# A two-layer hybrid decoder step: weight granules multiplied in three fp32r products, or once in float32

## What is computed

```python
for l in range(DEPTH):                                   # DEPTH = 2
    x = layer_norm(DN_ALPHA * x + 0.5 * swiglu(x, ffn1_w_in[l], ffn1_w_out[l]), ln1_g[l], ln1_b[l])
    proj = x @ w_in[l]                                   # 1024 x 2696
    f_r, f_s, f_g = jnp.split(proj, [R_PROJ, R_PROJ + S_PROJ], axis=-1)
    y_r = rwkv7_mixer(f_r, ...); y_s = swa(f_s, ...); y_g = gdn_mixer(f_g, ...)
    mix = jnp.concatenate([y_r, y_s, y_g], axis=-1) @ w_out[l]      # 1024 x 1024
    x = layer_norm(DN_ALPHA * x + mix, ln2_g[l], ln2_b[l])
    x = layer_norm(DN_ALPHA * x + 0.5 * swiglu(x, ffn2_w_in[l], ffn2_w_out[l]), ln3_g[l], ln3_b[l])
# swiglu: gate, up = split(x @ w_in (1024 x 5632)); (silu(gate) * up) @ w_out (2816 x 1024)
```

## Time and profile before

| | |
|---|---|
| median of 3 runs | 3039.74 us (3028.84 to 3040.9) |
| the profiled execution's own time | 3037.87 us |
| its span, first to last instruction | 3036.1 us |
| PE busy | 2744.6 us, 90% |
| DVE busy | 1652.3 us, 54% |
| ACT busy | 941.4 us, 31% |
| mean granted TensorE clock | 0.896 |

### The profile page before, as it was taken

How to read it: one execution, slowest core, us unless ns; L and a number is a source line. 1 busy time by engine, 2 the same in 40 slices (tenths; PEclk the granted TensorE clock), 3 DMA queues, 4 the chain that set the end, 5 groups by cost and what they waited for, 6 DMA issues and landing times.

```text
span 3036.1 us, 59313 instructions
## 1 busy us (share of the span) xinstructions
PE 2744.6 (90%) x23248; PEld 2565.4 (84%) x23248; DVE 1652.3 (54%) x2489; ACT 941.4 (31%) x1679; POOL 179.6 (6%) x186
## 2 busy tenths in 40 slices
PE   8999999978787799999999999998887688999995
PEld 8999998856565699999999999987665567999994
DVE  5666346745555356663366643565555543666533
ACT  4333233322212133332233332343222212433322
POOL 1030110000000020001100001000000002000010
PEclk9999999977676699999999999998686768999997
DMA  4842334200000223232222222421000012223221
GB/s 110 99 90 87 88 114 113 56 8 1 9 9 5 72 77 90 83 90 85 84 79 88 85 86 87 130 91 32 5 9 1 9 38 80 77 83 90 86 85 47
DMA packets 381441, 201.60 MB, mean 66 GB/s; under 512 B 41381, under 2 KB 378789, under 8 KB 380472
## 3 DMA queue, kind: packets, MB, share of 16 engines
q1 hardware_dynamic: 378872, 197.46, 22.6%
q0 software_dynamic: 2400, 1.82, 1.8%
HBM read 188.07 MB, written 13.34 MB: 66 GB/s over the span
## 4 chain that ended last, share of the span: by engine, by line
PE 80%; DVE 10%; issue 5%; ACT 4%; SPq 1%; DMA 0%; DVEq 0%; ACTq 0%; POOLq 0%; POOL 0%
PE ps L656 55%; PE ps L710 22%; DVE ar L1805 3%; DVE ar L1799 2%; ACT ar L1336 2%; SPq L517 1%; PE ps L1059 1%; PE ps L964 1%; ACT wh L1267 1%; DVE wl L1683 1%; DVE x L1713 0%; DVE x L1799 0%; DVE ar L1835 0%; DVE x L1711 0%; DVE xl L1790 0%
## 5 line engine op out<-in xcount | busy, mean ns | idle before, releaser
L1683 DVE TENSOR_TENSOR wl<-raws,wh 128x1024 fp32r<-128x1024 f32 x332 | 406.5, 1225 | 734.5 <-ACT wh L1267 730.5
L656 PE MATMUL ps<-xh,wh 128*128 128x272 f32 x3136 | 662.7, 293 | 43.8 <-DVE xl L1799 18.2
L656 PE MATMUL ps<-xh,wl 128*128 128x272 f32 x3136 | 656.3, 291 | 0.0
L656 PE MATMUL ps<-xl,wh 128*128 128x272 f32 x3136 | 654.8, 290 | 0.0
L710 PE MATMUL ps<-ar 64*64 64x64 f32 (+13 forms) x4984 | 495.3, 294 | 122.8 <-ACT ar L1336 38.2
L710 PEld LDWEIGHTS ps<-ar 64*64 64x64 f32 (+5 forms) x4984 | 370.1, 179 | 223.4 <-issue 64.0
L656 PEld LDWEIGHTS ps<-xh,wh 128*128 128x128 f32 x3136 | 502.1, 192 | 49.7 <-issue 26.5
L656 PEld LDWEIGHTS ps<-xl,wh 128*128 128x128 f32 x3136 | 502.0, 191 | 0.0
L656 PEld LDWEIGHTS ps<-xh,wl 128*128 128x128 f32 x3136 | 501.1, 191 | 0.0
L1267 ACT ACTIVATE wh<-raws 128x1024 fp32r<-128x1024 f32 x332 | 350.6, 1057 | 455.9 <-PE ps L656 430.6
L656 PE MATMUL ps<-hh,wh 128*128 128x272 f32 x1408 | 292.2, 289 | 0.0
(11 more groups left out here) (188 smaller groups left out, 2755.2 us busy)
## 6 DMA issues: line engine op xcount, KB each, us to landing
raws<-in_ffn_w_in SPq DMA_DIRECT2D x176, 512.0 KB, 3.7
raws<-in_ffn_w_out SPq DMA_DIRECT2D x64, 512.0 KB, 4.0
raws<-in_w_in SPq DMA_DIRECT2D x42, 512.0 KB, 3.6
raws<-in_ffn_w_out SPq DMA_DIRECT2D x32, 384.0 KB, 3.4
raws<-in_w_out SPq DMA_DIRECT2D x16, 512.0 KB, 4.1
x_kept<-x SPq DMA_DIRECT2D x2, 2176.0 KB, 10.2
x<-x_kept SPq DMA_DIRECT2D x2, 2176.0 KB, 7.9
ar<-in_consts SPq DMA_DIRECT2D x2, 1337.5 KB, 6.5
```

The costliest lines, as they stand in the source:

```text
L656: ins = pe.matmul(ps[:, bank + h, 0:n1 - h * NH], w[u % 2][:, k, :], a[:, k0 + k, h * NH:n1], start=(first and k == 0 and n == 0), stop=(l ...
L1683: dve.tensor_tensor(wl[u % 2][:, :, :], raw[u % 2][:, :, :], wh[u % 2][:, :, :].bitcast(F32), ALU.subtract).then_inc(sem("wl_done"), 1)
```

## The change

All granules and activations are plain float32. `raws` becomes a ring of four load buffers (`SLOTS`), TensorE reads the weights there and waits for the load itself; `wh`, `wl`, `xl`, `hl` and all code that makes them are gone. SP waits on `mm_done` of the granule that used the slot before. The mixer's input counts two granules that do not exist (`SKIP`), so that each stage begins at slot 0; the first two granules of `w_out` are loaded right after the last of the mixer's input, into slots 0 and 1, since odd head pairs keep rows in slots 2 and 3. `keep_busy` is taken out. DVE writes `hh` and the last step of each head straight into `xh`. FFN loops of SP and TensorE are unrolled to multiples of four granules.

```diff
-        xh = sb("xh", [P, KC, NX], F32R)
-        xl = sb("xl", [P, KC, NX], F32R)
-        raws = sb("raws", [P, 2, 8, P])
+        xh = sb("xh", [P, KC, NX])
+        raws = sb("raws", [P, SLOTS, 8, P])
...
             def load(lay, g, u, src):
-                sp.wait_ge(sem("wl_done"), at(lay, "wl_done", g + u - 1))
-                sp.dma_start(raw[u % 2][:, 0:src.shape[1], 0:src.shape[2]], src).then_inc(raw_in[u % 2], 16)
+                slot = u % SLOTS
+                sp.wait_ge(sem("mm_done"), at(lay, "mm_done", g + u - SLOTS + 1))
+                sp.dma_start(raw[slot][:, 0:src.shape[1], 0:src.shape[2]], src).then_inc(raw_in[slot], 16)
...
-            def granule(lay, g, u, nblocks, hi, lo, k0, bank, first, last, split_from=None):
-                pe.wait_ge(sem("wl_done"), at(lay, "wl_done", g + u + 1))
+            def granule(lay, base, n, u, nblocks, a, k0, bank, first, last, split_from=None):
+                slot = u % SLOTS
+                pe.wait_ge(raw_in[slot], (lay * slot_uses(NG, slot) + slot_uses(base, slot) + n + u // SLOTS + 1) * 16)
                 for k in range(nblocks):
                     if split_from is not None:
-                        pe.wait_ge(sem("xl_done"), at(lay, "xl_done", split_from + k + 1))
-                    for n, (w, a) in enumerate(((wh, hi), (wh, lo), (wl, hi))):
-                        for h in range(2):
-                            n1 = a.shape[2] if h else NH
-                            ins = pe.matmul(ps[:, bank + h, 0:n1 - h * NH], w[u % 2][:, k, :], a[:, k0 + k, h * NH:n1],
-                                            start=(first and k == 0 and n == 0), stop=(last and k == nblocks - 1 and n == 2))
+                        pe.wait_ge(sem("xh_done"), at(lay, "xh_done", split_from + k + 1))
+                    for h in range(2):
+                        n1 = a.shape[2] if h else NH
+                        ins = pe.matmul(ps[:, bank + h, 0:n1 - h * NH], raw[slot][:, k, :], a[:, k0 + k, h * NH:n1],
+                                        start=(first and k == 0), stop=(last and k == nblocks - 1))
...
-                def keep_busy(p, n):
-                    if p.q == 3:
-                        for _ in range(n):
-                            pe.matmul(ps[:, 3, 0:NH], xh[:, 2, 0:P], xh[:, 3, 0:NH], start=True, stop=True)
...
-            def split(lay, g, u):
-                n = g + u
-                act.wait_ge(raw_in[u % 2], lay * (NG // 2 * 16) + g * 8 + (u // 2) * 16 + 16)
-                act.wait_ge(sem("mm_done"), at(lay, "mm_done", n - 1))
-                act.activation(wh[u % 2][:, :, :], raw[u % 2][:, :, :], ACT.Copy).then_inc(sem("wh_done"), 1)
...
-            def split(lay, g, u):
-                dve.wait_ge(sem("wh_done"), at(lay, "wh_done", g + u + 1))
-                dve.wait_ge(sem("mm_done"), at(lay, "mm_done", g + u - 1))
-                dve.tensor_tensor(wl[u % 2][:, :, :], raw[u % 2][:, :, :], wh[u % 2][:, :, :].bitcast(F32),
-                                  ALU.subtract).then_inc(sem("wl_done"), 1)
...
-                tt(xl[:, 2:6, 0:SEQ], y_attn[:, :, 0:SEQ], xh[:, 2:6, 0:SEQ].bitcast(F32), ALU.subtract).then_inc(*tick("attn_l"))
...
-                        stt(y, y, 0.5, U[:, ZG, :], ALU.mult, ALU.mult).then_inc(*tick("y_final"))
+                        if q == 3:
+                            dve.wait_ge(sem("x_back"), at(lay, "x_back", 16))
+                        stt(final, y, 0.5, U[:, ZG, :], ALU.mult, ALU.mult).then_inc(*tick("head_l"))
...
-                    if q == 3:
-                        split(lay, BASE_WO, 0)
-                    dve.wait_ge(sem("head_h"), at(lay, "head_h", q + 1))
-                    ch = q if q < 2 else 4 + q
-                    tt(xl[:, ch, 0:NT], y, xh[:, ch, 0:NT].bitcast(F32), ALU.subtract).then_inc(*tick("head_l"))
```

More of the change, by code:

```diff
@@ L46 @@
 N_FFN_IN, N_FFN_OUT = 2 * FC, 3 * KC
+SLOTS = 4
+SKIP = -PC % SLOTS
 BASE_F1I = 0
@@ L49 @@
 BASE_PJ = BASE_F1O + N_FFN_OUT
-BASE_WO = BASE_PJ + PC
+BASE_WO = BASE_PJ + PC + SKIP
 BASE_F2I = BASE_WO + KC
@@ L53, with slot_uses @@
 NG = BASE_F2O + N_FFN_OUT
+assert all(b % SLOTS == 0 for b in (BASE_F1O, BASE_PJ, BASE_WO, BASE_F2I, BASE_F2O, NG))
+def slot_uses(base, slot):
+    return base // SLOTS - (base >= BASE_WO and slot >= SLOTS - SKIP)
 LAST_ROW = P - 1
@@ L265, in trunk @@
         x = sb("x", [P, KC, NT])
-        xh = sb("xh", [P, KC, NX], F32R)
-        xl = sb("xl", [P, KC, NX], F32R)
-        raws = sb("raws", [P, 2, 8, P])
[L269 to L273, removed]
+        xh = sb("xh", [P, KC, NX])
+        raws = sb("raws", [P, SLOTS, 8, P])
+        raw = [raws[:, s] for s in range(SLOTS)]
         gram_odd = sb("gram_odd", [P, GRAM_W])
@@ L334, in trunk @@
         passed = sem("passed")
-        raw_in = [sem("raw_in0"), sem("raw_in1")]
+        raw_in = [sem(f"raw_in{k}") for k in range(SLOTS)]
         for name in START:
@@ L556, in one_layer @@
                     load_proj(g)
+                for u in range(2):
+                    load(lay, BASE_WO, u, columns(w_mix, lay, (0, KC), u * P))
                 def put(dst, src, name="states_out"):
@@ L611, in one_layer @@
                         put(out("p_" + name, lay)[:, 0, 2 * c + hp, :, :].rearrange("a m n -> (a m) n"), src, "state_out")
-                with sp.Fori(1, KC // 2) as c:
-                    for u in range(2):
-                        load(lay, BASE_WO + c * 2, u, columns(w_mix, lay, (0, KC), c * (2 * P) + u * P))
+                for u in range(4, KC):
+                    load(lay, BASE_WO, u, columns(w_mix, lay, (0, KC), u * P))
+                    sp.sem_inc(passed, 1)
                 ffn_weights(lay, 1, BASE_F2I)
@@ L717, in proj_part @@
                         pe.sem_inc(passed, 1)
-                        pe.wait_ge(sem("wl_done"), at(lay, "wl_done", BASE_PJ + g + 1))
+                        pe.wait_ge(raw_in[g % SLOTS], (lay * slot_uses(NG, g % SLOTS) + slot_uses(BASE_PJ, g % SLOTS) + g // SLOTS + 1) * 16)
                     for k in range(k0, k1):
[L720 to L724, removed]
+                        for h in range(2):
+                            n1 = NX if h else NH
+                            ins = mm(ps[:, 2 * u + h, 0:n1 - h * NH], raw[g % SLOTS][:, k, :], xh[:, k, h * NH:n1],
+                                     start=(k == 0), stop=(k == KC - 1))
                     if k1 == KC:
-                        ins.then_inc(sem("mm_done"), 1)
+                        ins.then_inc(sem("mm_done"), 1 + SKIP if g == PC - 1 else 1)
                 def turn_caches():
@@ L1303, in ffn @@
                 g_cols(lay, 2 * ph, lay + (LN_SLOT[1] if ph == 0 else 1))
[L1305 to L1314 removed]
+                with act.Fori(0, KC // 2) as d:
+                    for u in range(2):
+                        squares(lay, 2 * ph, d * 2, u)
+                        z_high(lay, 2 * ph, lay + (LN_SLOT[1] if ph == 0 else 1), d * 2 + u)
             def g_cols(lay, n, slot):
                 act.wait_ge(sem("lnp_in"), 16 * LN_DMAS)
[L1319 removed]
+                act.activation(xh[:, :, NT:NX], affine_cols(slot), ACT.Copy)
             def squares(lay, n, c, u):
```

198 lines of the change are left out of this document (58 added, 140 removed).

## The result

| | before | changed |
|---|---|---|
| median | 3036.35 us (4 runs, 3028.84 to 3040.9) | 3380.16 us (4 runs, 3368.36 to 3384.87) |
| ratio, 95% interval | | 1.1129 (1.1091 to 1.1168) |
| the profiled execution, its span | 3037.87 us, 3036.1 us | 3380.69 us, 3378.8 us |

A forecast was written before the change was run, and what follows sets the result against it. The prediction took TensorE, 90% busy and without gaps in the FFN stages, as the bound. Its terms, +417 - 23 - 27 - 20 = +347 us on the profiled 3037.87 us, gave 3385 us, range 3346 to 3440.

The forecast's parts named there:

- Term A: TensorE's granules: 10368 float32 records at 228.6 ns, 2374 us in place of 1957, +417 us.
- the way to +652 us: TensorE's granules: each float32 matmul costs four fp32r records, +652 us, in all 3620 us; a rival at 5%.
- Term B: TensorE's granules: waits on the splits go with the splits and a ring of four, -23 us, bounds 0 and -25.6.
- Term C: Heads, finish(3) and the `w_out` start: keep_busy and split steps go, 13.7 us a layer, -27 us, bounds -10 and -40.
- keep_busy's -8 us a layer: finish(3): 12.7 us a layer of fillers on the chain go, 8 copy waits of about 0.5 us come back.
- The w_out hand-over: Last DVE step to TensorE's `w_out` start, 3.27 us: split and subtraction go, a bare hand-over stays, -2.7 us a layer.
- the 3 us a layer in the earlier heads: Earlier heads: ACT copies and DVE subtractions go, 3 us a layer taken of about 6.
- Term D: Mixer's input stage: 10 of 13.2 us a layer of TensorE idle time go, -20 us, bounds 0 and -26.
- Rivals 1 to 3: In the granules: float32 matmul costs four fp32r records (5%); clock falls (4%); one array pass a record, faster (3%).
- Rival 4: Heads and mixer's input: waits stay, a cold stretch without keep_busy eats the rest, 3455 us; 10%.

The follow-up runs named there:

- f32_with_splits: The kernel before with one plain float32 multiplication in place of three products; splits, two load buffers and keep_busy stay: 3421.39 us, ratio 1.1242.
- the half-column run: The changed kernel with 136 of 272 columns from the second block of a result on, in the FFNs and `w_out`: 2457.35 us.
- after_two_slots: The changed kernel with two load buffers in place of four, the w_out loads all waiting for the last head pair: 3423.81 us, ratio 1.1251.
- the run of its own: The kernel before without its 82 keep_busy filler matmuls, 41 a layer: 3037.16 us, ratio 0.9984.
- one product in the old frame: The kernel before with wh times xh alone, both low products left out: 2762.82 us, a single run.
- the two-product kernel: The kernel before without its third product, wl times xh: 2772.09 us, a single run.

## Why the prediction was right

The forecast was 3385 us; the median is 3380.16 and the profiled execution took 3380.69.

**Term A, +417 us: held.** Read by the same view it is 7552 x 229.4 + 2816 x 228.3 ns = 2375 us against 1957, +418. Eight records of norm_sums gave the rate to a nanosecond, f32_with_splits the same rate with all else unchanged. What was wrong in the way to +652 us was the price of a pass: a record that costs twice its columns costs as much as two passes of 113 ns, not two fp32r records of 126. The four passes of the Trainium skill, page "FP8 and Floating Point Precision", section "TensorE Precision Notes", agree with this as two in each of two records; the half-column run shows the cost per column, and the passes are read from it.

**Term B, -23 us: held in size, in mechanism only in part.** The rest columns of the FFNs, of `w_out`, the start and the end give -26.7. I had put it down to waits that go with the splits and the deeper ring. f32_with_splits keeps the splits and two buffers, and its FFN 1 is as fast: there the longer granule covers the splits. What taking them out gave is 4.1 us at each FFN 2 start (74.4 against 70.3 us) and 8.8 us at the layers' boundary (497.8 against 489.0), 17 us in all. Around the wait at this boundary the clock also stood at its lower level for some 10 us (0.70 granted from 1503 to 1520 us), in the changed kernel not at all (1.00). That four buffers cover every load was true; that two would, as the expectation of after_two_slots took from "a load lands in 4 us", was not.

**Term C, -27 us: too large, measured -12.** The failed step is keep_busy's -8 us a layer: 3.7 by the run of its own. I had taken its 12.7 us on the chain less eight waits of half a microsecond; ten waits of 0.4 us and one of 1.6 us came back, 5.6 us, and some 3 us of the difference stand in no wait. The w_out hand-over gave 2.0 of 2.7, because I had misread where it begins. Four steps run from 1039.06, not three:

```profile
1039.06 3.07 DVE L1805 SCALAR_TENSOR_TENSOR ar<-ar 128x544 f32<-128x544 f32 x4
```

The last one ends at 1042.13 and not at 1041.38, so 2.52 us lay between it and TensorE's start, and 0.56 us do after the change. Of the 3 us a layer in the earlier heads nothing can be seen: the piece before finish(3) went up 3.6 us in one layer and down 4.4 in the other, no more than it differs between traces. So -12 has an error of that size, and only finish(3) and its end, 5.5 us a layer, are measured.

**Term D, -20 us: too small, measured -37.** All 13.2 us a layer of waits went, where I took 10, and 5 to 6 us more that stand in no wait. The clock has them: the stage had a granted clock of 0.97 in 176 us, which is about 10 us at the lower level and so 5 us lost (an estimate: half of these 10 us), and it has 1.00 now. I had priced the waits and not the clock behind them. Some 70% of the term comes from the longer granule by itself.

C and D are wrong by +15 and -17 us and cancel; that the forecast lies within 5 us is luck, that it lies within some 20 is not. Rivals 1 to 3 fall with the rate (436 records in 100 us) and the clock of 1.00. Rival 4 had one thing right, that keep_busy's cover was in part needed, and is wrong by 75 us for the whole.

## What to carry to other kernels

Where one engine has no gap, the price of a change is the rate of its stream, and a handful of records of the new form anywhere in the old trace gives it; taking the splits and fillers away and deepening the ring gave 41 us here against 418 (3421.39 to 3380.16), and the longer granules covered another 35 by themselves. A wait on the bound engine can cost more than its own length, when the clock falls behind it: 5 us a layer on top of 13. Before taking a chain of helpers away, ask which bound lies under the present one: here the float32 form removed a bound that was not active (2763 us) and raised the one that was. A two-deep ring is judged by the slowest load in any stretch, not by the median: 9.2 us in one stage against 3.8 overall cost 20 us.

## What was not expected of the hardware

- An fp32r record of 272 columns takes 125.2 ns at full clock (126.1 where half of the records have 274), a float32 record of 136 columns, which by its cost counts twice, 115.7. Over the columns at 2.4 GHz the float32 record has 2 to 3 ns and the fp32r record 12. The Trainium skill, page "TensorE: Matmul & The Clock Gate", section "Back-to-back issue gap", gives N / 2.4 + 2.5 ns for a warm matmul by itself and says that in a stream of weight loads and matmuls both set the spacing. The float32 records here, which are such a stream, agree with the formula all the same when N is taken twice (115.8 and 229.2 ns); the fp32r records do not.
- A float32 record of 68 columns with a 128-column stationary operand takes 213 ns at the lower clock, where its columns alone would be 113 ns at 1.2 GHz. Something other than the moving columns sets a floor there. The 128 stationary columns taken twice at 1.2 GHz would be 213 ns, an estimate that no run here tests.
- When TensorE got gaps the clock fell: one product in the old frame had a mean granted clock of 0.723, and about half of its granules' records came some 227 ns apart instead of 126; the two-product kernel, whose time is the same but for 9 us, had 0.867. How much time the lower clock took back there is open.
